# Hybrid decoder step on one Trainium2 core: the output projection's first chunk multiplied by token halves, with its splits, the sample shares and the value-sum copy in another order

## What is computed

```
def diff_attn_sample(q, k_new, v_new, k_past, v_past, lam, table):   # the 8 sample tokens
    a = diff_probs(logits(q1, kp1, kn1), logits(q2, kp2, kn2), lam)  # softmax(l1) - lam * softmax(l2)
    return einsum(a[..., :P], v_past) + einsum(a[..., P:], v_new)

def even_mixer(h, ...):
    a_out = rmsnorm(attend(da_q, da_k, da_v), g_da) * (1.0 - lam_init)
    o, s_new = gla_recurrence(gq, g_k, g_v, log_a, gla_s0)
    o = rmsnorm(o, g_gla) * silu(g_og)
    mix = concatenate([a_out, o])
    return mix @ w_out, da_k, da_v, s_new
```

## Time and profile before

| | us |
|---|---|
| median of three runs | 1537.47 |
| lowest, highest | 1536.75, 1541.28 |
| the profiled execution's own time | 1539.73 |
| its span | 1537.9 |
| PE busy | 1401.2 (91%) |
| DVE busy | 880.8 (57%) |
| ACT busy | 514.8 (33%) |
| POOL busy | 328.8 (21%) |
| mean granted TensorE clock | 0.935 |

### The profile page before, as it was taken

How to read it: one execution, slowest core, us unless ns; L and a number is a source line. 1 busy time by engine, 2 the same in 40 slices (tenths; PEclk the granted TensorE clock), 3 DMA queues, 4 the chain that set the end, 5 groups by cost and what they waited for, 6 DMA issues and landing times.

```text
span 1537.9 us, 26186 instructions
## 1 busy us (share of the span) xinstructions
PE 1401.2 (91%) x11360; PEld 1268.1 (82%) x11360; DVE 880.8 (57%) x1161; ACT 514.8 (33%) x840; POOL 328.8 (21%) x267
## 2 busy tenths in 40 slices
PE   5999957788687698999999999899989999999997
PEld 5999833345344398999999999899989999999996
DVE  4799868866776526535344353689556344353443
ACT  3422254533342424212222132468443222121232
POOL 1567668775755100000000000000000000000000
PEclk8999968987767799999999999999999999999998
DMA  8788688998978721322322322222213223223211
GB/s 294 253 293 284 239 302 335 394 370 297 332 300 303 273 83 56 110 83 84 111 83 91 102 83 83 83 83 84 84 58 102 89 83 110 83 83 110 83 56 56
DMA packets 126857, 249.34 MB, mean 162 GB/s; under 512 B 5251, under 2 KB 107415, under 8 KB 110096
## 3 DMA queue, kind: packets, MB, share of 16 engines
q0 software_dynamic: 18432, 134.23, 23.2%
q1 hardware_dynamic: 105180, 109.46, 22.1%
q10 hardware_dynamic: 3132, 3.98, 0.9%
HBM read 239.99 MB, written 7.73 MB: 161 GB/s over the span
## 4 chain that ended last, share of the span: by engine, by line
PE 56%; issue 26%; DVE 9%; POOL 4%; ACT 3%; DMA 2%; POOLq 0%; another core or an unknown queue 0%; ACTq 0%; SPq 0%; DVEq 0%
PE PS L1891 45%; POOL PROD L698 2%; DMA KV<-in_cache_v,CIDX 2%; DVE SC L1361 2%; PE PS L2098 2%; PE PS L2182 1%; PE PS L1875 1%; PE PS L2240 1%; POOL KV L765 1%; DVE SC L1373 1%; DVE PROD L1371 1%; DVE ST L1600 1%; PE PS L2203 1%; DMA XIN<-in_x_prompt 1%; PE PS L2085 1%
## 5 line engine op out<-in xcount | busy, mean ns | idle before, releaser
L1891 PE MATMUL PS<-H_hi,W_hi 128*128 128x260 f32 x1936 | 398.4, 287 | 14.9 <-DVE H_lo L1336 9.7
L1891 PE MATMUL PS<-H_hi,W_lo 128*128 128x260 f32 x1936 | 393.5, 285 | 0.0
L1891 PE MATMUL PS<-H_lo,W_hi 128*128 128x260 f32 x1936 | 393.4, 285 | 0.0
L1891 PEld LDWEIGHTS PS<-H_hi,W_hi 128*128 128x128 f32 x1936 | 303.3, 191 | 19.2 <-issue 14.4
L1891 PEld LDWEIGHTS PS<-H_hi,W_lo 128*128 128x128 f32 x1936 | 302.2, 191 | 0.0
L1891 PEld LDWEIGHTS PS<-H_lo,W_hi 128*128 128x128 f32 x1936 | 301.9, 191 | 0.0
L1294 DVE TENSOR_TENSOR W_lo<-RAW,W_hi 128x2048 fp32r<-128x2048 f32 x90 | 206.2, 2291 | 116.9 <-ACT W_hi L823 116.8
L823 ACT ACTIVATE W_hi<-RAW 128x2048 fp32r<-128x2048 f32 x89 | 169.9, 1909 | 268.6 <-PE PS L1891 265.5
L1891 PE MATMUL PS<-U_hi,W_lo 128*128 128x260 f32 x1024 | 206.4, 283 | 0.0
L1891 PE MATMUL PS<-U_lo,W_hi 128*128 128x260 f32 x1024 | 206.0, 283 | 0.0
L1891 PE MATMUL PS<-U_hi,W_hi 128*128 128x260 f32 x1024 | 206.0, 282 | 0.0
(11 more groups left out here) (312 smaller groups left out, 1500.1 us busy)
## 6 DMA issues: line engine op xcount, KB each, us to landing
RAW<-in_w_up SPq DMA_DIRECT2D x32, 1024.0 KB
RAW<-in_w_down SPq DMA_DIRECT2D x32, 1024.0 KB
RAW<-in_w_in_even SPq DMA_DIRECT2D x13, 1024.0 KB
RAW<-in_w_in_odd SPq DMA_DIRECT2D x8, 1024.0 KB
RAW<-in_w_out_even SPq DMA_DIRECT2D x4, 1024.0 KB
RAW<-in_w_out_odd SPq DMA_DIRECT2D x4, 1024.0 KB
x_saved<-X ACTq DMA_DIRECT2D x1, 2080.0 KB, 12.4
X<-x_saved SPq DMA_DIRECT2D x1, 2080.0 KB, 7.9
```

Source lines behind the costliest of these rows:

```text
L1891: t = MM_(PS[:, 2 * bank + j, 0:HALF], w[:, ch.slot, k, cols], x[:, k, half], start=k == 0 and n == 0, stop=k == KT - 1 and n == 2)
```

## The change

- PM has a second buffer pair in memory where PJ's tiles 12 and following lie (`PM_AT`); parts 8 to 15 use it, and POOL zeroes it ahead of part 8. So W_lo's slot of the first chunk no longer shares memory with a PM that is in use.
- ScalarE: `squares_of(23)` and `split_hi(C_OUT0)` stand ahead of the two stores of the prompt state; the two exponentials of the sample softmax follow the sixth of the eight H_hi copies, with a root of one column behind them; so the OG copy comes directly after the eighth H_hi copy.
- VectorE: the last row sums and `split_lo(C_OUT0)` stand ahead of `inverse_norm(23)`; the sample maxima stand behind the fourth `mixed_lo`, the shares behind the eighth.
- POOL: `power(23)` is issued behind value chunk 55, no longer behind 57.
- TensorE: the first chunk is multiplied half by half (`halves_apart`): half 0 of the first output tile, the sum of the sample squares, half 0 of the second tile, and then, behind `new_ready`, half 1 of both.

```diff
--- before.py
+++ after.py
@@ -199,7 +199,7 @@
     GVT = sb("GVT", [P, 4, 512], F32, r_w + 8000)
     PR = sb("PR", [P, 2, 2, 512], F32, r_w + 16192)
     PM_LEAD = 24
-    PM = sb("PM", [P, 2, PM_LEAD + 16 * 32], F32, r_w + 24384)
+    PM_AT = [sb(f"PM{i}", [P, 2, PM_LEAD + 16 * 32], F32, at) for i, at in enumerate((r_w + 24384, r_1 + 12 * TB))]
     KDM = sb("KDM", [P, 8, P], F32, r_w + 28672)
     XL = sb("XL", [P, 2, 2, T], F32, r_raw)
     BC = sb("BC", [P, 2, SEQ], F32, r_raw + 8320)
@@ -701,10 +701,15 @@
         def weights(part):
             b, half = divmod(part, 2)
+            PM = PM_AT[part // 8]
             if part == 0:
                 po.wait_ge(tiles_done, first_tile(C_OUT0))
                 nc.gpsimd.memset(PM[:], 0.0).then_inc(pm_zeroed, 1)
                 po.wait_ge(pm_zeroed, 1)
+            if part == 8:
+                po.wait_ge(kd_ready, 1)
+                nc.gpsimd.memset(PM[:], 0.0).then_inc(pm_zeroed, 1)
+                po.wait_ge(pm_zeroed, 2)
             if part >= 2:
                 po.wait_ge(v_used, 4 * (part - 1))
             po.wait_ge(soft_done, b + 1)
@@ -713,7 +718,7 @@
         K_IN_UNITS = sum(UNIT_STEPS) + sum(IN_STEPS) + sum(PRE_STEPS)
         POWERS_BEFORE_K = {K_IN_UNITS: (14, 15), **{K_IN_UNITS + 2 * u + 2: (15 + u,) for u in range(1, 7)}}
-        POWER_BEHIND_V = {**{2 * u + 1: u - 1 for u in range(1, 15)}, 53: 22, 57: 23}
+        POWER_BEHIND_V = {**{2 * u + 1: u - 1 for u in range(1, 15)}, 53: 22, 55: 23}
         def power(u):
@@ -1049,10 +1054,11 @@
                 A(OT[:, par], PS[:, par, P:2 * P], ACT.Copy).then_inc(go_copied, 1)
             slot(GLA_SLOT + 2 * u + 1)
         slot(GLA_SLOT + 16)
+        squares_of(23)
+        split_hi(Chunk(C_OUT0))
         act.wait_ge(st_ready, 64)
         for hp in range(2):
             act.dma_start(o["gla_prompt"][hp], ST[:, hp, state(3, 8)]).then_inc(state_sent, 16)
-        squares_of(23)
         normalise(23)
         normalised(23)
@@ -1065,11 +1071,12 @@
             else:
                 act.wait_ge(hf_ready, 8 + q - 3)
                 A(H_hi[:, q, 0:SEQ], HTMP[:, q % 2], ACT.Copy).then_inc(hhi_ready, 1)
-
-        act.wait_ge(exp_asked, 4)
-        A(E1[:], E1[:], ACT.Exp)
-        A(E2[:], E2[:], ACT.Exp).then_inc(exp_given, 1)
-        split_hi(Chunk(C_OUT0))
+            if q == 5:
+                act.wait_ge(exp_asked, 4)
+                A(E1[:], E1[:], ACT.Exp)
+                A(E2[:], E2[:], ACT.Exp).then_inc(exp_given, 1)
+                A(SPT[:, 0, 0:1], EPSC[:, 0:1], ACT.Sqrt)
+
         past_output(1)
         act.wait_ge(new_held, 1)
@@ -1607,8 +1614,9 @@
             slot(GLA_SLOT + 2 * u + 1)
             k_chunks(max(steps - 2, 0))
             clamp(16 + u)
+        slot(GLA_SLOT + 16)
+        split_lo(Chunk(C_OUT0))
         inverse_norm(23)
-        slot(GLA_SLOT + 16)
         slot(GLA_SLOT + 17)
         def gated(q):
@@ -1624,6 +1632,29 @@
             ve.wait_ge(hhi_ready, 8 + q + 1)
             V.tensor_tensor(H_lo[:, q, 0:SEQ], PJ[:, q, 0:SEQ] if q < 4 else HTMP[:, q % 2], H_hi[:, q, 0:SEQ].bitcast(F32),
                             ALU.subtract).then_inc(h_ready, 1)
+
+        mp, zp, sn = MP[:], ZP[:], SN[:].rearrange("p b h c -> p (b h c)")
+        parts = lambda t: t[:].rearrange("p (b h c) -> p c h b", h=4, c=2)
+
+        def sample_maxima():
+
+            ve.wait_ge(smz_done, 1)
+            V.tensor_copy(MP[:], PS[:, 5, 256:320])
+            link(V.tensor_copy(ZP[:], PS[:, 5, 320:384]))
+            link(V.tensor_tensor(MM[:], mp, sn, ALU.max))
+            V.tensor_tensor(E1[:], mp, MM[:], ALU.subtract)
+            V.tensor_tensor(E2[:], sn, MM[:], ALU.subtract).then_inc(exp_asked, 1)
+
+        def sample_shares():
+
+            ve.wait_ge(exp_given, 4)
+            link(V.tensor_tensor(ZZ[:], zp, E1[:], ALU.mult))
+            link(V.tensor_tensor(ZZ[:], ZZ[:], E2[:], ALU.add))
+            link(V.reciprocal(ZZ[:], ZZ[:]))
+            z1 = ZZ[:].rearrange("p (x c) -> p c x", c=2)[:, 1]
+            link(V.tensor_scalar(z1, z1, LAM[:, 2:3], None, ALU.mult))
+            V.tensor_tensor(E1[:], E1[:], ZZ[:], ALU.mult)
+            link(V.tensor_tensor(E2[:], E2[:], ZZ[:], ALU.mult))
         ve.wait_ge(nev_done, 32)
         ve.wait_ge(v_sent, 64)
@@ -1633,23 +1664,9 @@
             mixed_lo(q)
             if q in (4, 5):
                 gated(q + 2)
-
-        mp, zp, sn = MP[:], ZP[:], SN[:].rearrange("p b h c -> p (b h c)")
...
-        link(V.tensor_tensor(E2[:], E2[:], ZZ[:], ALU.mult))
+            if q == 3:
+                sample_maxima()
+        sample_shares()
         past_output(1)
         ve.wait_ge(pvt_ready, 2)
         for c in range(2):
@@ -1664,7 +1681,6 @@
         ve.wait_ge(go_s_ready, 2)
         by_tile = lambda t: t[:].rearrange("p (k b) -> p k b", k=KT)
         V.tensor_scalar(by_tile(MM), PJ[:, 0:KT, SEQ:T], -SQUARE_OVERFLOWS, SQUARE_OVERFLOWS, ALU.max, ALU.min).then_inc(new_held, 1)
-        split_lo(Chunk(C_OUT0))
         ve.wait_ge(new_root, 1)
         link(V.reciprocal(ZZ[:], ZZ[:]))
         link(V.tensor_scalar(E1[:], PS[:, 6, 0:KT * N_SAMPLE], SQUARE_OVERFLOWS ** 2 / 256, 1.0 / 32, ALU.is_lt, ALU.mult))
@@ -1883,14 +1899,14 @@
                 t = MM_(SPREAD[:, g], IDENT[:, 32 * g:32 * g + 1].to_broadcast([P, P]), INVERSE, start=True, stop=True)
             t.then_inc(rs_spread, 1)
-        def step(ch, i, bank, k, hi, lo):
+        def step(ch, i, bank, k, hi, lo, which=(0, 1)):
             cols = slice(P * i, P * i + P)
             for n, (w, x) in enumerate(((W_hi, hi), (W_hi, lo), (W_lo, hi))):
-                for j, half in enumerate(halves):
-                    t = MM_(PS[:, 2 * bank + j, 0:HALF], w[:, ch.slot, k, cols], x[:, k, half],
+                for j in which:
+                    t = MM_(PS[:, 2 * bank + j, 0:HALF], w[:, ch.slot, k, cols], x[:, k, halves[j]],
                             start=k == 0 and n == 0, stop=k == KT - 1 and n == 2)
-            if k == KT - 1:
+            if k == KT - 1 and 1 in which:
                 t.then_inc(tiles_done, 1)
         def products(ch, hi, lo, ready=None, after=None, together=False):
@@ -1924,9 +1940,9 @@
         def set_ready(m):
             return lambda k: pe.wait_ge(h_ready, 8 * m + k + 1)
-        def stage(c0, count, m):
+        def stage(c0, count, m=None):
             for j in range(count):
-                products(Chunk(c0 + j), H_hi, H_lo, set_ready(m) if j == 0 else None)
+                products(Chunk(c0 + j), H_hi, H_lo, set_ready(m) if j == 0 and m is not None else None)
         def opening(opened, c0, m):
@@ -2095,7 +2111,7 @@
                     pe.wait_ge(pvt_ready, 1)
                 for pos in range(4):
                     at = PM_LEAD + 32 * (4 * (n % 4) + pos) - 8 * (b % 4)
-                    t = MM_(PS[32 * pos:32 * pos + 32, 4, :], PM[:, part % 2, at:at + 32], KV[i % RING][:, pos, :],
+                    t = MM_(PS[32 * pos:32 * pos + 32, 4, :], PM_AT[part // 8][:, part % 2, at:at + 32], KV[i % RING][:, pos, :],
                             start=n % 32 == 0, stop=n % 32 == 31)
                 t.then_inc(v_used, 1)
@@ -2217,10 +2233,29 @@
         pe.wait_ge(gs_v_used, N_SAMPLE)
         pe.wait_ge(hf_ready, 12)
-        pe.wait_ge(new_sq, 1)
-        MM_(PS[:, 6, 0:KT * N_SAMPLE], ONES[:], MM[:], start=True, stop=True).then_inc(new_summed, 1)
-        pe.wait_ge(new_ready, 1)
-        stage(C_OUT0, 4, 1)
+
+        def sample_squares():
+
+            pe.wait_ge(new_sq, 1)
+            MM_(PS[:, 6, 0:KT * N_SAMPLE], ONES[:], MM[:], start=True, stop=True).then_inc(new_summed, 1)
+
+        def halves_apart(ch):
+
+            pe.wait_ge(w_lo_ready, ch.ready)
+            for i in range(2):
+                pe.wait_ge(banks_free[ch.par[i]], ch.banks_free[i])
+                for k in range(KT):
+                    pe.wait_ge(h_ready, 8 + k + 1)
+                    step(ch, i, ch.par[i], k, H_hi, H_lo, (0,))
+                if i == 0:
+                    sample_squares()
+            pe.wait_ge(new_ready, 1)
+            for i in range(2):
+                for k in range(KT):
+                    step(ch, i, ch.par[i], k, H_hi, H_lo, (1,))
+
+        halves_apart(Chunk(C_OUT0))
+        stage(C_OUT0 + 1, 3)
         sum_squares(1)
         spread(1)
         mlp(0, C_MLP0, 2)
```

14 lines of the change are left out of this document (removed).

## The result

The changed kernel takes **1524.91 us** (median of 4 runs, 1520.74 to 1528.88) where the kernel before takes 1539.38 in the same comparison (4 runs, 1536.75 to 1542.33): ratio 0.9904, 95% interval 0.9881 to 0.9926. The prediction was 1526.0 with a range of 1523.9 to 1531.0, and "faster" at 0.94. Its profiled execution takes 1528.88 us with a span of 1526.8.

What follows compares the result with a forecast made beforehand. A serial chain from the value chunks' end to the output projection was taken as the bound. 9.7 us from the start plus 2.8 from the clock less 0.6 of holds, taken as 11.5, gave 1526.0 us, range 1523.9 to 1531.0.

Steps and rivals of the forecast that it cites:

- The start of the projection: TensorE's first projection matmuls start at 525.0, not 534.71, 9.7 us earlier, with both weight splits off the chain.
- The inverse norm: VectorE's last inverse norm, now behind W_lo's split, comes at 512.6 where it was 512.24: 0.4 us later.
- The clock: TensorE's granted clock stays at 1.00 from 520 on, saving the projection's cold start of 2.8 us.
- The holds: TensorE's short waits around the first half, for the sample squares and new_ready, cost 0.6 us in all.
- The value sums: Value chunks end 0.4 us later, at 523.15, but OG ends at 524.0, where it ended at 526.4.
- The sum: Projection end: 9.7 us from the start, 2.8 from the clock, less 0.6: -11.9, taken as -11.5; chance 0.57.
- the cover of the gathers: Last gathers, issued about 1.1 us later, fill engines until 519.4; TensorE wants the last buffer at 521.9: covered by 1.4.
- rival C: Sample chain stays the bound through later gathers, a cold clock or a later weight load; gain under 4.6 us; chance 0.04.
- my own sign: Wrong if the projection starts after 527, TensorE waits over 1 us for squares or new_ready, or the shift shrinks.
- Rival A: Clock falls between value chunks and first half; coming back costs 1.7 to 3.5 us; gain 8.0 to 9.8; chance 0.24.
- rival B: Prompt rows come 3 to 4 us late, H_hi copies waiting for the later stores; gain about 8; chance 0.13.
- rival D: Projection's 24 matmuls in a row into one bank cannot overlap: 16.0 us more, 4.5 us slower overall; chance 0.02.

Runs made afterwards that it cites:

- e10: The changed kernel unedited, timed again on another run's chip against the kernel before: 1526.51 us, ratio 0.9929.
- e4: The changed kernel with W_lo's split of the first chunk behind the last inverse norm instead of ahead of it: 1533.39 us, ratio 0.9949.
- e7: The changed kernel with both splits of the first weights back at their places before the change, halves still apart: 1534.64 us, ratio 0.9977.
- e8: The changed kernel with X's reload held until the last two value gathers land and W_lo behind the last inverse norm: 1529.09 us, ratio 0.9927.
- e9: The changed kernel with X's reload held for the last gathers and W_lo's split behind the sixth gated tile: 1531.94 us, ratio 0.9954.
- e3: The kernel before with 31 unused matmuls in TensorE's three waits ahead of the projection, to keep the clock up: 1537.2 us, ratio 0.9982.
- e1: The changed kernel unedited, first repeat against the kernel before: 1530.05 us, ratio 0.9932.
- e5: The changed kernel with SyncE's reload of X held until the last two value gathers have landed: 1527.82 us, ratio 0.9927.
- e6: The changed kernel with X's reload held and the last norm's power back behind value chunk 57: 1530.2 us, ratio 0.9931.

## Why the prediction was right, and where it was not

- **The start of the projection.** Predicted 9.7 us earlier; +29.0 to +19.6 is 9.4, and 10.2 in e10. Both splits left the stretch behind the value sums, as said; W_lo is on the chain ahead of the inverse norm where no gather is late.
- **The inverse norm.** Predicted +0.4 us; it is +0.1. It starts where W_lo ends, as predicted; with W_lo elsewhere it is at +3.8 (e4, e7, e8, e9), since the earlier power alone brings it there.
- **The clock.** Predicted 1.00 and 2.8 us. After has 1.00, and its projection takes 46.55 us for 48.74, 2.2 less, with the sum of squares inside. e3 gives 2.4 for the projection alone and 2.9 with the fold.
- **The holds.** Predicted 0.6; none in after, and some 0.2 in e10 ahead of the small sum. From start to end 46.55 us for 384 matmuls at 0.120 = 46.1 and the small sum. ScalarE has the squares at 529.48, ahead of the first half's end at 530.24.
- **The shares.** Predicted to end where they ended; +19.7 for +20.2, because VectorE's wait of 0.5 us for the exponentials went as well; my sum had left it in. PVT: predicted 2.6 us earlier, +19.9 for +22.8 is 2.9.
- **The value sums.** Predicted 2.4 us earlier, OG +18.0 for +20.1 is 2.1. In after it is the last gather that sets it, 0.72 us late.
- **The table load.** Predicted 1.3 us and no more: 1.28, and the next activation starts 0.01 us behind its end. The Trainium skill (ScalarE: Activation LUTs, What ACT_TABLE_LOAD costs) adds a drain of some 1.38 us; this trace does not show it, and the seventh H_hi held nobody.
- **The sum.** -11.9 worked out and -11.5 taken; -11.6 in the part that the change touches. Small misses cancel in it: e10, without the wait for the gather, has -12.2. And that the first median, 1524.91, lies 1.1 us from the forecast is in part luck: e1's is 4.1 above it, 1530.05, still inside the range.

**The step that did not hold** is the cover of the gathers: "the last gathers are issued about 1.1 us later ... covered by 1.4 us". The issue is 1.4 later, since one of them is slowed by W_lo, which I had not counted. The cover was read too large: 519.4 is where the gathers stop filling the engines, not where the last one has landed. In before, q0 has its last packets in 520.5 to 521, +14.8 to +15.3, and TensorE wants that buffer at +16.1, some 1 us later. In after one stands as late as 524 to 524.5, beside packets of q1, whose reload of X was issued at 522.90. Before in 520.5 to 521, then after in 524 to 524.5 (packets, MB, share):

```profile
q0 software_dynamic: 2, 0.01, 4.0%
```

```profile
q1 hardware_dynamic: 7, 0.12, 133.1%
q0 software_dynamic: 1, 0.00, 0.1%
```

In e5 (reload held) and e10 (reload just behind them) the last are gone by +15.7. So the 0.72 us of after may come of the reload as well as of the late issue; these rows do not part the two.

And the cover was measured in a picture that the change can leave: I took TensorE's need of the last buffer from the earlier trace rows, 48 matmuls in 7.5 us, which is a row of the low clock for more than half its length. In e1 the first 40 would have ended at +13.2 without a wait, 2.9 us sooner than 522.77 - 0.94 in before (+16.1; 0.94 is the last chunk at the high clock). SyncE's reload follows the first 32, and my own prediction has a weight load "directly behind X's reload", which I checked only against the matmul that wants it, not against the gather that it shares the engines with. In e1 the last gather is issued at 517.65 and its chunk starts at 529.95, 12.3 us later; in after it is 8.8.

That is rival C by its words ("the later gathers or a cold clock delay the last value sum as well") and by its price: "under 4.6", and e1's part is 77.76 - 73.84 = 3.9 us shorter. By my own sign, a start later than 527 (+21.3), e1 is an execution in which I am wrong. I gave C 0.04. It stands in one of three profiles of the changed kernel, so as a chance for a single execution it looks far too small. It does not carry the median. Taken by their ratios, the three comparisons give 1539.38 x 0.0096 = 14.8 us, 1538.32 x 0.0068 = 10.5 and 1539.35 x 0.0071 = 10.9 of gain, against a forecast of 11.5. Rival A's mechanism was seen in e9 (and over part of e6's first half), in e9 at 2.0 us, within the 1.7 to 3.5 that I had allowed; rival B not at all (the first H_hi starts 2.42 us behind the inverse norm in both kernels); rival D is excluded: 0.120 us per matmul with 24 in a row in one bank.

## What to carry to other kernels

Two serial stretches side by side hide each other's worth: removing either brings little (3.7 and 5.6 us in the profiles here), removing both brings more than the two added (11.6). Where a cover is the distance between a transfer's landing and its consumer, work it out at both levels of the consumer's clock, and ask what its finishing early sets off; here a gather's last packets were held up under a bulk load that started a moment sooner. Take more than one profile before a wait in it is called the kernel's: here the same program showed 0, 0.72 and 7.0 us of waits for the same gathers. And split the span at an event ahead of the edit, or the scatter of the 500 us before it is read as the edit's.
